# Attention and linear-attention value products of a decoder kernel, each split into four column tiles of TensorE

## What is computed

```python
# softmax attention, for each head; the weights p and the values v
p = softmax(scores)
out = einsum('bhqk,bkhd->bqhd', p, v)

# linear recurrence, for each head; the scores are made in levels of blocks
o_intra = einsum('bhts,bhsv->bhtv', scores, v)
```

## Time and profile before

| | |
|---|---|
| Median of the runs | 2271.99 us (2271.87 to 2272.09) |
| Profiled execution, its own time | 2273.14 us |
| Span of the trace of that execution | 2271.3 us |
| TensorE matmul busy | 2256.1 us, 99% of the span, 12989 matmuls |
| TensorE weight load busy | 2031.0 us, 89%, 12989 loads |
| VectorE busy | 1552.7 us, 68% |
| ScalarE busy | 1297.7 us, 57% |
| Granted TensorE clock, mean | 0.999 of full |
| DMA, mean over the span | 202 GB/s |

### The profile page before, as it was taken

How to read it: one execution, slowest core, us unless ns; L and a number is a source line. 1 busy time by engine, 2 the same in 40 slices (tenths; PEclk the granted TensorE clock), 3 DMA queues, 4 the chain that set the end, 5 groups by cost and what they waited for, 6 DMA issues and landing times.

```text
span 2271.3 us, 33030 instructions
## 1 busy us (share of the span) xinstructions
PE 2256.1 (99%) x12989; PEld 2031.0 (89%) x12989; DVE 1552.7 (68%) x1765; ACT 1297.7 (57%) x1741; POOL 12.9 (1%) x18
## 2 busy tenths in 40 slices
PE   9999999999999999999999999999999999999998
PEld 7898998888999988889999999988999999998887
DVE  6576577775766777787786677866666766765555
ACT  6444576454555764666765567555655655654444
POOL 0000000000000000000000000000000000000000
PEclk9999999999999999999999999999999999999999
DMA  9645557666545584655555546576666666667664
GB/s 322 212 161 172 169 182 280 230 235 196 167 149 186 192 296 153 224 185 176 177 194 178 184 169 204 194 270 212 205 202 204 197 200 205 197 216 249 203 203 149
DMA packets 130540, 459.91 MB, mean 202 GB/s; under 512 B 13864, under 2 KB 20560, under 8 KB 128464
## 3 DMA queue, kind: packets, MB, share of 16 engines
q1 hardware_dynamic: 129392, 451.43, 59.4%
q0 software_dynamic: 848, 6.30, 0.8%
q10 hardware_dynamic: 144, 0.07, 0.0%
HBM read 449.35 MB, written 8.40 MB: 202 GB/s over the span
## 4 chain that ended last, share of the span: by engine, by line
PE 97%; DVE 1%; DMA 1%; ACT 1%; issue 0%; SPq 0%; DVEq 0%; ACTq 0%
PE banks L317 91%; PE banks L437 1%; PE banks L417 1%; PE banks L402 1%; PE banks L381 1%; PE banks L409 0%; DVE wl L650 0%; DMA w_bc<-in_norm_mix_post 0%; DMA early<-in_kv_t 0%; ACT wh L483 0%; PE banks L449 0%; PE banks L460 0%; PE banks L461 0%; PE banks L459 0%; PE banks L425 0%
## 5 line engine op out<-in xcount | busy, mean ns | idle before, releaser
L650 DVE TENSOR_TENSOR wl<-raw,wh 128x1024 fp32r<-128x1024 f32 x774 | 940.9, 1222 | 497.9 <-ACT wh L483 495.3
L483 ACT ACTIVATE wh<-raw 128x1024 fp32r<-128x1024 f32 (+1 forms) x777 | 813.7, 1052 | 519.4 <-PE banks L317 441.2
L317 PE MATMUL banks<-xx,wh 128*128 128x512 f32 (+1 forms) x3760 | 858.1, 380 | 0.0
L317 PEld LDWEIGHTS banks<-xx,wh 128*128 128x128 f32 (+1 forms) x3760 | 688.3, 189 | 92.1 <-issue 1.0
L317 PEld LDWEIGHTS banks<-xx,wl 128*128 128x128 f32 x3712 | 455.4, 192 | 14.0
L317 PE MATMUL banks<-xx,wl 128*128 128x256 f32 x3712 | 465.0, 276 | 0.0
L317 PE MATMUL banks<-wh,xx 128*128 128x512 f32 x1504 | 360.1, 380 | 0.0
L317 PEld LDWEIGHTS banks<-wh,xx 128*128 128x128 f32 x1504 | 282.7, 189 | 39.6
L317 PE MATMUL banks<-wl,xx 128*128 128x512 f32 x752 | 196.1, 379 | 0.0
L317 PEld LDWEIGHTS banks<-wl,xx 128*128 128x128 f32 x752 | 142.1, 189 | 20.1
L317 PE MATMUL banks<-wh,yy 128*128 128x512 f32 x416 | 98.4, 379 | 0.0
(11 more groups left out here) (283 smaller groups left out, 1785.3 us busy)
## 6 DMA issues: line engine op xcount, KB each, us to landing
raw<-in_w_in_f SPq DMA_DIRECT2D x304, 512.0 KB, 3.3
raw<-in_w_ffn_f SPq DMA_DIRECT2D x160, 512.0 KB, 3.5
raw<-in_w_ffn_down SPq DMA_DIRECT2D x88, 512.0 KB, 4.3
raw<-in_w_in_t SPq DMA_DIRECT2D x80, 512.0 KB, 3.4
raw<-in_w_out_t SPq DMA_DIRECT2D x64, 512.0 KB, 4.5
raw<-in_w_o_t SPq DMA_DIRECT2D x32, 512.0 KB, 4.6
raw<-in_kv_f SPq DMA_DIRECT2D x16, 512.0 KB, 3.9
raw<-in_w_up_a_f SPq DMA_DIRECT2D x16, 512.0 KB, 3.4
```

Source lines behind the costliest of these rows:

```text
L317: return self.e.matmul(bank, stationary, moving, start=start, stop=stop, skip_group_check=True)
L483: self.e.activation(hi, source, ACT.Copy).then_inc(done.sem, 1)
L650: self.e.tensor_tensor(lo, source, hi.bitcast(f32), ALU.subtract).then_inc(done.sem, 1)
```

## The change

Every product in values and linear_values is split by the columns of the stationary operand: four matmuls with 32 stationary columns each, whose outputs go to partitions 0 to 31, 32 to 63, 64 to 95 and 96 to 127 of the same columns of the same bank. The moving operand is the same 128 columns for all four. Order of heads and key tiles, waits and the one signal at the end are as before.

```diff
                 for h in range(4):
                     for kt in range(nt):
                         pt = a.pt[:, (h * nt + kt) * P:(h * nt + kt + 1) * P]
-                        i = self.e.matmul(banks[4][:, h * P:(h + 1) * P], a.v(kt, h), pt, start=(kt == 0), stop=(kt == nt - 1))
+                        for c in range(0, P, 32):
+                            i = self.e.matmul(banks[4][c:c + 32, h * P:(h + 1) * P], a.v(kt, h)[:, c:c + 32], pt, start=(kt == 0),
+                                              stop=(kt == nt - 1))
                 i.then_inc(done.sem, 1)
...
-                    self.e.matmul(b[:, c:c + P], a.v(0, h), a.acc[:, a0:a0 + P], start=True, stop=True)
-                    self.e.matmul(b[:, c + P:c + S], a.v(0, h), a.acc[:, ao:ao + P], start=True, stop=False)
-                    i = self.e.matmul(b[:, c + P:c + S], a.v(1, h), a.acc[:, a1:a1 + P], start=False, stop=True)
+                    for o, t, n, start, stop in ((c, 0, a0, True, True), (c + P, 0, ao, True, False), (c + P, 1, a1, False, True)):
+                        for r in range(0, P, 32):
+                            i = self.e.matmul(b[r:r + 32, o:o + P], a.v(t, h)[:, r:r + 32], a.acc[:, n:n + P], start=start, stop=stop)
                 i.then_inc(done.sem, 1)
```

## The result

The kernel became slower by 0.28%: 2278.36 us (median of 9 runs, 2277.49 to 2280.63) against 2272.14 (9 runs, 2271.87 to 2273.22), ratio 1.0028 with a 95% interval of 1.0017 to 1.0038, +6.2 us. Forecast were 2278.6 and a range of 2275 to 2288. The profiled execution took 2278.36 us, with a span of 2276.6.

A forecast was written before the change was run, and what follows sets the result against it. TensorE, busy 99% of the span, was taken to bound the kernel. Passes 0, going in and out of the tiles 6.2 and tiles out of step 0.4 made +6.6 us on 2272.0: 2278.6 us, range 2275 to 2288.

The forecast's parts named there:

- What bounds: Whole kernel: TensorE, busy 99% of the span, paces it, so a call's longer time moves the end by the same amount.
- No change per product: All 152 products of values and linear_values: eight narrow passes take the present time, 0.223 us a product, so 0 us.
- The bound of 1.5 us of gain: Lower bound for the 304 passes: 32-column loads take away at most 0.005 us each, 1.5 us of gain.
- The seam: Going into and out of the tiles at each of the 20 calls: 0.31 us each, 6.2 us, up to 7.8.
- Tiles out of step: In each call the last tile starts after the first: 0.02 us a call, 0.4 us in all, at most 3.8.
- Handed over too slowly: Rival, in the calls: eight passes need 0.253 us a product; +11.2 us in all, 2283.2 us; chance 0.12.
- Two at a time or strict order: Rival, in the calls: two tiles together or strictly ordered starts, four passes' time a product; +40.5 us, 2312.5; chance 0.08.
- No overlap: Rival, in the calls: eight passes in a row, 0.894 us a product; 2380.4 us, or 2373.8 without tiles; chance 0.05.
- Taken up by idle time: Rival: TensorE's 3.5 us idle between 766 and 1081 us absorbs delay; +1.6 us, 2273.6, not slower; chance 0.07.
- the 0.0317 us that I had kept as an end of the range: Upper bound on narrow passes in the calls: one every 0.0317 us, 0.253 us a product, 4.6 us more.

The follow-up runs named there:

- the kernels with one and with two seams a call: Against the kernel before: only each call's first product in four column tiles, 2278.71 us; heads 0 and 2 in tiles, 1 and 3 whole, 2285.42 us.
- the level kernels: Kernel before, values whole, second block's levels s = 16, 8, 4 in column tiles: four tiles 2270.20 us, two tiles of 64 columns 2270.17 us.

## Why the prediction was right

- **What bounds.** TensorE paces the kernel where the calls stand, and every microsecond of theirs came through to the end: 5.9 us in the calls' frames, +6.2 by the medians.
- **No change per product.** Right, and the term was taken 0.7 us too high: 0.109 us a group instead of 0.1117. The bound of 1.5 us of gain held it, though the reading behind that bound was wrong. The prediction took 0.107 us a pass from the step with 72 moving columns for the pace of the load, and 0.111 for the moving side. But 1.71/16 takes in a shorter first and a shorter last step: in the timeline of the step at 1029.78 us the starts between are 0.112 apart, as with 96 and with 128 moving columns. So it is the other way about: whole products go at 0.1117, set by the load as far as the runs tell, and tiles, where the moving side sets it, at 0.109. Four tiles stream the same columns as fast as two, which no row had shown.
- **The seam.** Right. It was put at 0.31 us from the one step with 32 stationary columns. The change's frames, 0.29 us on the average of the calls of eight products, plus 16 x 0.0025 for the shorter passes, make 0.33, with 0.02 of tiles out of step in it; the kernels with one and with two seams a call give the same. 20 x 0.33 - 0.7 = 5.9, the sum of the frames. The forecast of 6.6 lies above it by the passes alone, which it took as unchanged; the medians, 6.2, lie between, so that they come within 0.4 of the forecast is in part luck.
- **Tiles out of step.** Right. Four tiles start within 0.03 us, as the two 64-row tiles had done.
- **Handed over too slowly** fell with the level kernels (0.016 us a matmul) and with the 64-column tiles.
- **Two at a time or strict order** fell with the first group of four starts. The Trainium skill, TensorE: Matmul & The Clock Gate, section "The mechanism", has matmuls start in program order; here the first pass of the fourth tile starts 0.02 us after the first of the first tile, ahead of three second passes that come before it in the program. With two products of a tile in a row it holds for whole products:

```profile
148.42 0.34 PE L418 MATMUL banks<-sm_pt,mv 128*32 128x128 f32 x4
```

  These four start by 148.47 us. One tile starts a pass only every 0.11 us, so they are of four tiles, although each tile's second product stands ahead of the next tile's first in the program. That holds only within the short queue of each tile. With eight passes in a row this rival's mechanism, a later tile kept behind an earlier one, is there, and costs 32 us more than the change by the frames, 34 by the medians.
- **No overlap** fell with it.
- **Taken up by idle time** fell too: TensorE still waits 2.8 us for VectorE before the block levels, and between 766 and 1083 us after it is busy 313.53 of 317 us, 3.5 us idle as before.

```profile
PE banks L451 <- DVE lke L791: 2.8, 2, 1.5
```

What remains argued is why a seam costs what it does. Its way in is 0.09 to 0.10 us in every frame; the way out is the larger part. The loads (PEld) show where the time goes. The call's first load before; then, after, the last whole matmul ahead of the call, the call's first load, its last four matmuls and the first whole load behind it:

```profile
146.95 0.19 PEld L417 LDWEIGHTS banks<-sm_pt,mv 128*128 128x128 f32 x1
```

```profile
145.82 0.28 PE L317 MATMUL banks<-xx,wl 128*128 128x256 f32 x1
146.03 0.11 PEld L418 LDWEIGHTS banks<-sm_pt,mv 128*32 128x32 f32 x1
147.69 0.29 PE L418 MATMUL banks<-sm_pt,mv 128*32 128x128 f32 x4
147.91 0.19 PEld L317 LDWEIGHTS banks<-xx,wl 128*128 128x128 f32 x1 [0.20 <-issue]
```

Before, a load starts with the matmul ahead of it (146.95 us both). At a seam it starts 0.20 us after it, both ways: 145.82 to 146.03, and 147.71, the last of the four, to 147.91. On the way out the next whole matmul is late once more, 0.21 us after the first instead of 0.11. So no load is made ahead across the change of shape, in or out. What makes the load wait, no kernel here varied; it stays open.

A seam costs the same where the load of 128 columns paced the step: with 0.1117 and 0.063 us a pass the level with 72 columns saves 16 x 0.0487 = 0.78 us in passes and 0.45 in its frame (0.46 by the rounded lines), which leaves 0.33, as in the change.

## What to carry to other kernels

Splitting a full 128-column product of float32 with 128 moving columns into column tiles gives next to no speed (0.109 instead of 0.1117 us a pass), and costs about 0.3 us each time TensorE goes from whole products to tiles and back; count these changes, not the matmuls. Tiles pay where the load of 128 stationary columns is longer than the moving stream (here up to 96 moving columns, with 16 passes to earn the seam back), or where narrow outputs can be put beside each other (the block step, 0.63 us instead of 1.04). Then the tiles must alternate in the program: here four passes in a row of one tile cost 0.9 us more than two by the frames, eight cost 32.

## What the runs showed of the hardware that I had not expected

- Four column tiles, each streaming the same 128 columns of all 128 partitions, lose nothing to one another: 64 matmuls in 1.95 us, as 16 whole ones before.
- A matmul with its load can be handed over every 0.016 us (64 in 0.99 us), far faster than the 0.0317 us that I had kept as an end of the range.
- A tile's queue holds one running and three waiting passes, and a full queue blocks the other tiles' passes behind it: runs of 2, 4, 8 and 16 passes of a tile take 1.95, 2.02, 4.33 and 5.96 us for the same 64 matmuls.
- Whole float32 products go at 0.1117 us a pass with 72, 96 or 128 moving columns alike; in stationary columns of 32 or 64, in turn, those with 72 go at 0.063.
- A change between whole products and column tiles costs 0.33 us for the way in and out together (0.35 with tiles of 64 columns), whatever paced the products before; the next load starts 0.20 us after the matmul ahead of it instead of with it.
